# Modulation columns 16 to 18 made in the first MLP, at one chunk per two chunks of weights, instead of beside the second mixer

## The reference

```
h = rms_norm(x, norm_mlp[l])
x = x + jnp.square(jax.nn.relu(h @ w_up[l])) @ w_down[l]        # 2048 -> 8192 -> 2048
```

```
sh_m, sc_m, gt_m, sh_f, sc_f, gt_f = split(silu(c) @ w_mod[l] + b_mod[l], 6)        # w_mod: 2048 x 12288
csh_m, csc_m, ... = split(silu(c_ctx) @ w_mod[l] + b_mod[l], 6)
h_lat = modulate(rms_norm_2(x, norm_mix_g[l]), sh_m, sc_m)
h_ctx = modulate(rms_norm_2(y, norm_mix_g[l]), csh_m, csc_m)
...                                        # second mixer: h_lat @ w_in, h_ctx @ w_in, scan, attention
x = x + gt_m * (concatenate([hg_lat, at_lat]) @ w_out[l])
x = x + gt_f * swiglu(modulate(rms_norm_2(x, norm_ffn_g[l]), sh_f, sc_f), w_gate_up[l], w_down[l])
```

## Time and profile before

| | |
|---|---|
| median of 3 runs | 2678.79 us (2674.7 to 2679.52) |
| the profiled execution | 2677.59 us, span 2675.8 us |
| mean granted TensorE clock | 0.998 |
| TensorE busy | 2627.8 us, 98% of the span |
| VectorE busy | 1790.9 us, 67% |
| ScalarE busy | 1279.1 us, 48% |
| read and written | 572.51 MB, mean 214 GB/s |

### The profile page before, as it was taken

How to read it: one execution, slowest core, us unless ns; L and a number is a source line. 1 busy time by engine, 2 the same in 40 slices (tenths; PEclk the granted TensorE clock), 3 DMA queues, 4 the chain that set the end, 5 groups by cost and what they waited for, 6 DMA issues and landing times.

```text
span 2675.8 us, 34219 instructions
## 1 busy us (share of the span) xinstructions
PE 2627.8 (98%) x13536; PEld 2199.1 (82%) x13536; DVE 1790.9 (67%) x2476; ACT 1279.1 (48%) x1774; POOL 30.4 (1%) x58
## 2 busy tenths in 40 slices
PE   8899999999999999999999999999999999999999
PEld 7799889888888888778878788888788888888887
DVE  5667665676788888866866775667666666454555
ACT  5434564554534434455655455555454444434433
POOL 1000000000000000000000000000000000000000
PEclk9999999999999999999999999999999999999999
DMA  8786655577787788876777754554577777566665
GB/s 258 236 262 204 202 165 177 151 250 253 253 267 254 257 263 259 269 247 185 238 218 234 230 183 133 163 152 127 158 212 252 251 251 223 180 196 189 188 193 177
DMA packets 301872, 572.51 MB, mean 214 GB/s; under 512 B 20156, under 2 KB 28640, under 8 KB 301584
## 3 DMA queue, kind: packets, MB, share of 16 engines
q1 hardware_dynamic: 297744, 558.11, 66.5%
q0 software_dynamic: 3792, 12.14, 1.6%
q10 hardware_dynamic: 176, 0.07, 0.0%
HBM read 568.15 MB, written 2.10 MB: 213 GB/s over the span
## 4 chain that ended last, share of the span: by engine, by line
PE 87%; DVE 4%; DMA 4%; ACT 3%; issue 2%; SPq 0%; DVEq 0%; ACTq 0%
PE ps L1775 25%; PE ps L1777 24%; PE ps L1776 24%; PE ps L1769 2%; DMA raw<-in_w_in 2%; PE ps L1771 2%; PE ps L1770 2%; PE ps L1717 2%; DVE wlo L2402 1%; ACT whi L2084 1%; PE ps L1871 1%; DMA raw<-in_w_down 1%; DVE acc L2420 1%; DMA raw<-in_w_mod 1%; ACT Eb L2171 0%
## 5 line engine op out<-in xcount | busy, mean ns | idle before, releaser
L2402 DVE TENSOR_TENSOR wlo<-raw,whi 128x1024 fp32r<-128x1024 f32 x857 | 1043.8, 1223 | 692.3 <-ACT whi L2084 683.5
L2084 ACT ACTIVATE whi<-raw 128x1024 fp32r<-128x1024 f32 x857 | 902.9, 1058 | 1032.0 <-PE ps L1777 283.7
L1775 PE MATMUL ps<-whi,th 128*128 128x512 f32 (+1 forms) x3128 | 1238.5, 396 | 11.4 <-DVE wlo L2402 9.1
L1777 PE MATMUL ps<-whi,tl 128*128 128x512 f32 (+1 forms) x3128 | 1213.8, 388 | 0.0
L1776 PE MATMUL ps<-wlo,th 128*128 128x512 f32 (+1 forms) x3128 | 1212.5, 388 | 0.0
L1775 PEld LDWEIGHTS ps<-whi,th 128*128 128x128 f32 x3128 | 588.4, 188 | 140.6 <-DVE wlo L2402 16.3
L1777 PEld LDWEIGHTS ps<-whi,tl 128*128 128x128 f32 x3128 | 587.9, 188 | 123.1
L1776 PEld LDWEIGHTS ps<-wlo,th 128*128 128x128 f32 x3128 | 588.9, 188 | 114.8 <-issue 1.4
L2420 DVE SCALAR_TENSOR_TENSOR acc<-raw,silc,acc 128x512 f32<-128x512 f32 x480 | 344.5, 749 | 31.0 <-DMA raw<-in_w_mod 26.3
L1769 PE MATMUL ps<-th,whi 128*128 128x256 f32 (+1 forms) x656 | 191.8, 292 | 4.6 <-DVE ckT L2388 2.4
L1770 PE MATMUL ps<-th,wlo 128*128 128x256 f32 (+1 forms) x656 | 186.7, 285 | 0.0
(11 more groups left out here) (318 smaller groups left out, 1293.5 us busy)
## 6 DMA issues: line engine op xcount, KB each, us to landing
raw<-in_w_in SPq DMA_DIRECT2D x240, 512.0 KB, 4.1
raw<-in_w_down SPq DMA_DIRECT2D x216, 512.0 KB, 4.7
raw<-in_w_mod SPq DMA_DIRECT2D x192, 512.0 KB, 3.9
raw<-in_w_gate_up SPq DMA_DIRECT2D x176, 512.0 KB, 3.8
raw<-in_w_up SPq DMA_DIRECT2D x128, 512.0 KB, 4.0
raw<-in_w_out SPq DMA_DIRECT2D x64, 512.0 KB, 4.0
raw<-in_xattn_wkv SPq DMA_DIRECT2D x16, 512.0 KB, 3.7
raw<-in_xattn_wq SPq DMA_DIRECT2D x8, 512.0 KB, 3.5
```

The lines of the kernel that those rows point to most:

```text
L1775: pe.matmul(p, xh, wh[:, c, c0:n], start=a and (form == "rows" or tb == 0), stop=False, skip_group_check=True)
L1777: ins = pe.matmul(p, xl, wh[:, c, c0:n], start=False, stop=z, skip_group_check=True)
L2084: self.e.activation(t.his[g % NHI][:, 0:n], t.raws[j % NRAW][:, 0:n], ACT.Copy).then_inc(*s.hi.up(g))
L2402: self.e.tensor_tensor(t.los[j % NRAW][:, 0:n], t.raws[j % NRAW][:, 0:n], t.his[g % NHI][:, 0:n].bitcast(F), ALU.subtract).then_inc(*s.lo. ...
```

## The change

At the first MLP the rate goes from 0.4 to 0.5 modulation chunks for each chunk of weights, and groups 16 to 18 are put behind groups 0 to 7 in `todo`. The second mixer is left with group 19, at 0.1 instead of 0.3. The list of chunks holds the same chunks as before, in another order.

```diff
         self.acc_after[2] = self.acc_after[3] = scrX
-        self.rate = 0.4
-        self.todo = self.todo + [(j, kc) for j in range(8) for kc in range(8)]
+        self.rate = 0.5
+        self.todo = self.todo + [(j, kc) for j in [*range(8), *range(16, 19)] for kc in range(8)]
...
-        self.mods_start(16, 20, 0.3)
+        self.mods_start(19, 20, 0.1)
```

## The result

Before 2677.7 us in the median of 20 runs, after 2681.6 (2677.3 to 2689.9, 20 runs): ratio 1.0016, 95% interval 1.0009 to 1.0023. That is slower by 0.16%: within the 0.2% that the prediction took for its bound, and with an interval that reaches just over it. 2685 was forecast from 2678.8; the measured change is +4 us against +6. The profiled executions stand at 2675.8 and 2681.3, 5.5 us apart.

The account below looks back on a forecast made before the run. The prediction took TensorE to bound the kernel, so only its waits count. Terms +7 (down products), +2 (up), +1.5 (last down product), +0.5 (start) and -5 (mixer) gave +6 us: 2685, range 2673 to 2698, likeliest case 2680 to 2690.

Parts of the forecast that it names:

- The bound: Whole kernel: TensorE is busy 98% at full clock, so only waits taken from or given to it change the time.
- The chain in the two down products: First MLP, groups 0 to 7: load to low part takes 11.20 us against 10.47 available, so TensorE stalls; +7 us.
- A's low part: `wlo` of the first of two weight chunks per modulation load; VectorE makes it only after that load's four adds.
- the residual adds: Two VectorE adds ending each product, 1.20 us, fall between two low parts: 0.7 late, a third kept, eight times, 1.9.
- The up products and the start of the MLP: First MLP: chain 10.1 us fits with 0.37 spare, but disturbances cost +2 in up products; the start costs +0.5.
- `down(2)` with POOL's loads: Last down product with modulation: context, gain and mask loads make throughput decide; +1.5 us, between 0 and +4.
- an m of two operations: Modulation chunk of groups 13 to 15 or 16 to 18: chain 9.9 us in down products against 10.47, so it hides.
- The mixer: Second mixer: 24 loads and 48 VectorE operations go, so TensorE's waits and half clock shrink; -5 us, bounds 2 to 8.
- The sum: Whole kernel: the MLP's losses less the mixer's gain make +6 us, 2685 on the median.
- VectorE has room: Rival: chain fits if loads land under 4.4 us; MLP costs at most 1, mixer gives 7 to 8; 2672, chance 0.19.
- The loads crowd: Rival: denser loads land later, 5.6 us in down and 4.5 in up products; +15 us, 2694, chance 0.17.
- A step short: Rival: the last modulation chunk is left for mods_finish and TensorE waits up to 7 us more; 2692, chance 0.04.

Follow-up runs that it names:

- e6: Changed kernel with seven raw buffers, three high-part buffers and a lookahead of two instead of six, four and three: 2668.7 us, ratio 0.9969.
- e12: Changed kernel with six raw buffers as before, but three high-part buffers and a lookahead of two: 2690.9 us, ratio 1.0053.
- e3: Changed kernel with VectorE's adds into acc for groups 0 to 7 over only 128 of 512 columns, same loads: 2673.8 us, ratio 0.9998.
- e11: Kernel before, with POOL's loads of the gain and masks held back until the third down product is through: 2672.5 us, ratio 0.9990.
- e2: Changed kernel with POOL's loads of the final gain and masks held until TensorE has done the third down product: 2674.4 us, ratio 0.9996.
- e10: Changed kernel with seven raw buffers, three high-part buffers, a lookahead of two, and POOL's gain and mask loads held back past the third down product: 2664.0 us, ratio 0.9955.
- e8: Kernel before, adds into acc for groups 16 to 19 over only 128 of 512 columns: one execution, span 2674.4 us, mixer 400.6 against 403.1.
- e9: Kernel before with seven raw buffers, three high-part buffers and a lookahead of two: 2675.1 us, ratio 0.9998.

## Why the prediction was right, and where its sum was luck

**The bound.** Right. All that moved was waits of TensorE, most of a microsecond or less and one of 4.4 with the lower clock behind it; the page shows nothing.

**The chain in the two down products: +7 forecast, 11.3 between the stages, of which 1.3 are column sums.** Right in mechanism, too small by 3, and nearer than its terms. With six buffers the chain is too long (e6 and e12 differ in the seventh buffer: 90.2 against 95.2), shortening VectorE's adds is enough to mend most of it (e3), and A's low part is what is late. But the waits for `wlo` had been put at 9.7 us (0.24 in each of 32 periods, 7.8, and 1.9 for the residual adds) and came to 5.1, in 10 places. Two terms that were missing made up for it.
First, a stop costs more than its idle time. With the same 432 products, `down(0)` has TensorE busy for 92.5 us with stops and 90.3 without, `down(1)` 92.7 and 90.2: 4.6 us more, with 13 stops that the trace lists. At each of them some 0.3 us can be read off: products that start 0.23 apart are 0.39 long, so 0.16 of overlap is lost at a stop, and the second product behind it starts 0.34 after the first instead of 0.23 (788.50 and 788.84). The rest are delays too short for the list. The Trainium skill ("TensorE: Matmul & The Clock Gate", Step-by-step: what each phase is for) says that one product's drain overlaps the next one's fill; the 0.39 and the 0.23 agree with that.
Second, the column sums. I wrote that sums and transposes would hold TensorE for a microsecond here and there and give about 3 us back. They did the reverse: the copy waited on ScalarE behind a `whi` whose load was late, 2.0 us in three places of these two products (4.7 in seven of the whole MLP).

**The up products and the start of the MLP: +2.5 forecast, +1.9 measured.** The size is luck. By the instructions in the trace 1.4 of the 1.9 are column sums, which the forecast had left out; for the stalls that it had priced 0.5 us is left. Loads landed in 3.9 us in the median there, and the chain fits.

**`down(2)` with POOL's loads: +1.5 forecast, between 0 and 4; +7.0 measured.** This is the step that failed. I let an m of two operations hide (9.9 us against 10.47) and priced nothing but the added bytes (0.8 us at 371 GB/s; a tenth of an m in each of the 7.4 chunks of those 20 us is 0.4 MB, so 1.0). Neither held. POOL's 2.2 MB go out in a burst of 2.9 us, the weights behind it land in 9.2 us, and TensorE stands still for 4.4 us where the earlier trace rows already had 3.1, and then runs at the lower clock: 13 products in 5.6 us, which at 0.23 each would take 3.0. But the burst costs the kernel before almost as much: 4.4 us (e11) against 5.3 (e2), so only 0.9 of the 7.0 is the burst's. The other 6.1 stay without it, in waits for the copy of a column sum (2.7 us), for low parts (1.8 against 0.8) and for `stg` (1.7). There the two-operation m doesn't hide: weights land in 5.6 us in the median instead of the 5.1 of the sum, and from A's issue to the end of its low part it takes 8.1 us (7.1 in e11), where the forecast had 9.9 less 2.72, 7.2. With seven buffers and late loads nothing of it is left (e10), and 304 GB/s go through without a wait. How the 6.1 divide between landing, the copies and the ring no run shows.

**The mixer: -5 forecast, between -2 and -8; -14.2 measured, of which 2.1 are column sums: -12.** Under-sized by more than half, and outside its range. All 8.3 us of idle time went. The other 3.8 are the half clock (seven products up to 0.25 us further apart, 1.4 in all) and what the stops cost beyond their idle time. The 1.5 at L2284 that I had excluded as ScalarE's own went too: a load came late, one step further back than I had looked. And shorter adds get only 2.5 of 14.2 (e8), so the length of the adds is the smaller part; between the number of loads and the places of the m no run tells.

**The sum.** +18 and -12 give the +6 that I wrote as +11 and -5. Two errors of 7 us cancelled, and that is luck. The time was right and the two terms were not; on the sizes of e9 and e6, where the first term is small, the second decides and the change gains.

**The rivals.** VectorE has room: false with six buffers, true with seven, where it is 93% busy without a wait. The Trainium skill ("Perfetto Trace Analysis", Identifying the Most-Contended Engine) would judge by occupancy; here 87 to 88% with six buffers stalls TensorE and 93% with seven doesn't, so occupancy decided nothing. The loads crowd: not in `down(0)` and `down(1)` (e3; down loads land in 5.3 us in the median of the MLP, up loads in 3.9, where this rival wanted 5.6 and 4.5), in part in `down(2)`. A step short: no. Issues of modulation loads from 515 to 1197 us in the changed kernel, against the earlier trace rows (count, size, median us to landing):
```profile
raw<-in_w_mod SPq DMA_DIRECT2D x112, 512.0 KB, 5.2
```
All 112 that the count wanted.

**What stays open.** What makes the 6.1 us of `down(2)` that late loads don't remove; why a lookahead of two with three high-part buffers, and which of the two, shortens the start by 14 to 18 us while it lengthens the mixer by 10; and whether a ring of six fails because it is two periods long, or only because it is short. A ring of seven is both longer and no multiple of the period, and no other length was run.

## What to carry to other kernels

Work that rides along in a ring of buffers isn't priced by the load of any engine, but by the time from a buffer's release to the need of what it brings, against the chain of everything in between, riders included. Try one buffer more before moving the work; the same move was worth +0.16% with one set of sizes and -0.3% with the other. To say what a burst of loads costs a change, take it away on both sides: here it cost both kernels nearly the same. When a sum of small terms comes out right, compare it stage by stage: here each half was off by 7 us, more than the whole change.

## What the runs showed of the hardware

- A TensorE stop of 4.4 us was followed by a granted clock of 0.50 for 5.6 us or more. One of 1.9 us in `down(2)` of e9 was followed by some 1.5 us of products 0.23 us apart and then by 0.51 for 3.3 us. The one of 1.7 us at `stg` in `down(2)` of the changed kernel was not followed by it, nor were those of up to 1.0 us in `down(0)` and `down(1)` (granted clock 1.00). The Trainium skill ("TensorE: Matmul & The Clock Gate", What's actually happening) says that idleness throttles and activity releases, and these rows agree.
- A stop of TensorE costs about 0.3 us beyond its idle time (0.16 and 0.11 at each; with the delays too short for the list 4.6 us in two products with 13 stops), and the wait view doesn't show it.
- The DMA engines carried 304 GB/s over 90 us without making TensorE wait (e10, seven buffers). With 2.2 MB of POOL's issued within 2.9 us, the landing of a 512 KB load of weights went from 5 to 9.2 us at 390 GB/s and a DMA share of 1.02, and TensorE stopped for 4.4 us, at a mean of 283 GB/s over the product. The burst cost 4.4 us before the change and 5.3 after it.
- Engines take their instructions in the order of the program here: a copy of 0.4 us on ScalarE that was ready stood behind a `whi` that waited 1.52 us for its load, and TensorE waited 0.65 us for the copy.
